# Neighbourhood attention on 416 keys a query tile in place of 512, its latent tokens stored by grid column, with turned edges of 32 queries, a third output tile begun early and one eviction moved ahead

## The reference

```python
def neighbourhood_attention(q, k, v, kc, vc, rpb):      # 16 heads of 64; kc, vc: 256 context tokens
    n_rows = S // GRID_W                                # 256 // 64 = 4, so kr = 4: all rows are seen
    q_cols = np.arange(GRID_W).reshape(n_cb, NA_QCOLS)
    win_start = np.clip(q_cols - NA_COLS // 2, 0, GRID_W - NA_COLS)   # 16 columns around the query
    ...
    s = jnp.where(col_valid, q_k * scale + bias, NEG_INF)
    s_ctx = jnp.einsum('bjqhd,bkhd->bhjqk', qr, kc) * scale
    p = softmax_f32(jnp.concatenate([s_ctx, s], -1))
    return p[..., :n_ctx] @ vc + p[..., n_ctx:] @ vb
```

## Time and profile before

| | us |
|---|---|
| median of three runs | 1891.6 |
| the profiled execution's own time | 1889.94 |
| its span, first to last instruction | 1888.2 |
| TensorE busy | 1735.9 (92%) |
| VectorE busy | 935.7 (50%) |
| ScalarE busy | 371.4 (20%) |

### The profile page before, as it was taken

The page is one execution under the profiler, slowest core; times in us unless marked ns, Lnnn a source line. Parts: engine busy times, 40 slices in busy tenths (PEclk is TensorE's granted clock), DMA queues, the critical chain, the costliest instruction groups (busy, mean ns, idle before and its releaser), DMA issues.

```text
span 1888.2 us, 33088 instructions
## 1 busy us (share of the span) xinstructions
PE 1735.9 (92%) x14018; PEld 1356.1 (72%) x14018; DVE 935.7 (50%) x1988; ACT 371.4 (20%) x884; POOL 0.2 (0%) x4
## 2 busy tenths in 40 slices
PE   7999999999999999999999999999999776667676
PEld 4455686888888887666888888788888655545554
DVE  1488878666667428788454412477433211111112
ACT  0343413121120014222211102212412100000001
POOL 0000000000000000000000000000000000000000
PEclk9999999999999999999999999999999988888888
DMA  9523342222231216654244543322296999999997
GB/s 384 207 113 125 144 179 71 79 80 86 86 145 36 109 47 207 205 184 173 90 163 149 208 171 134 134 81 121 90 380 267 426 427 428 429 428 429 428 428 314
DMA packets 35968, 395.72 MB, mean 210 GB/s; under 512 B 4000, under 2 KB 7072, under 8 KB 14368
## 3 DMA queue, kind: packets, MB, share of 16 engines
q1 hardware_dynamic: 35872, 394.33, 52.6%
HBM read 393.26 MB, written 1.05 MB: 209 GB/s over the span
## 4 chain that ended last, share of the span: by engine, by line
PE 78%; DMA 18%; DVE 2%; ACT 1%; issue 1%; SPq 0%; DVEq 0%; ACTq 0%
PE bank L636 19%; DMA arena<-w_moe 16%; PE bank L1918 13%; PE bank L1627 9%; PE bank L689 5%; PE bank L3683 3%; PE bank L2168 3%; PE bank L2214 2%; PE bank L934 2%; PE bank L3449 1%; PE bank L2164 1%; DMA ring<-w_moe 1%; PE bank L1235 1%; PE bank L843 1%; PE bank L2226 1%; PE bank L2775 1%
## 5 line engine op out<-in xcount | busy, mean ns | idle before, releaser
L636 PE MATMUL bank<-layer_input,ring 128*128 128x256 f32 x1152 | 253.1, 380 | 0.0
L636 PEld LDWEIGHTS bank<-layer_input,ring 128*128 128x128 f32 x1152 | 217.4, 190 | 31.6 <-issue 2.7
L3683 PE MATMUL bank<-arena 128*32 128x128 f32 x2008 | 82.1, 331 | 49.0 <-DMA arena<-w_moe 48.7
L1627 PE MATMUL bank<-arena,ring 128*128 128x256 f32 x544 | 121.7, 379 | 0.0
L3835 DVE TENSOR_TENSOR arena<-arena,bank 128x128 f32<-128x128 f32 x32 | 9.2, 288 | 218.4 <-PE bank L3683 218.4
L1918 PE MATMUL bank<-arena 128*128 128x256 f32 x504 | 115.7, 379 | 0.0
L3683 PEld LDWEIGHTS bank<-arena 128*32 128x32 f32 x2008 | 69.7, 134 | 62.0 <-DMA arena<-w_moe 59.0
L1627 PEld LDWEIGHTS bank<-arena,ring 128*128 128x128 f32 x544 | 103.2, 190 | 14.4 <-issue 0.4
L1918 PEld LDWEIGHTS bank<-arena 128*128 128x128 f32 x504 | 95.7, 190 | 13.2 <-DVE arena L2047 0.2
L689 PE MATMUL bank<-arena,ring 128*128 128x256 f32 x452 | 99.1, 380 | 0.9 <-DVE arena L2410 0.6
L689 PEld LDWEIGHTS bank<-arena,ring 128*128 128x128 f32 x452 | 85.6, 190 | 13.3 <-issue 1.0
(11 more groups left out here) (519 smaller groups left out, 2742.1 us busy)
## 6 DMA issues: line engine op xcount, KB each, us to landing
arena<-w_moe SPq DMA_DIRECT2D x45, 2048.0 KB, 25.8
ring<-w_moe SPq DMA_DIRECT2D x45, 2048.0 KB, 26.5
ring<-w_ffn_in SPq DMA_DIRECT2D x22, 2048.0 KB, 8.1
ring<-w_proj SPq DMA_DIRECT2D x7, 3072.0 KB, 10.3
ring<-w_ada_late SPq DMA_DIRECT2D x8, 2560.0 KB, 9.3
ring<-w_ffn_out SPq DMA_DIRECT2D x7, 2816.0 KB, 9.4
ring<-w_na_pair SPq DMA_DIRECT2D x5, 2048.0 KB, 8.1
arena<-w_far SPq DMA_DIRECT2D x16, 512.0 KB, 5.8
```

The costliest lines, as they stand in the source:

```text
L636: last = pe.matmul(out, a, b, start=(k == 0), stop=(k == len(lhs) - 1))
L1627: last = eng.matmul(out, w[:, k * P:(k + 1) * P], x[:, k, :], start=(start and k == 0), stop=(stop and k == half - 1), skip_group_check=True)
L3683: ins = eng.matmul(bank[x][group[q], 0:P], xe[:, k, SLOTS * e:SLOTS * e + SLOTS], weight(e, first, last, (x * KT + k) * FE + q * P, P), st ...
```

## The change

- **Order of the latent tokens.** `split_out` of the first FFN writes the 256 latent columns of `self.A` so that column c and row r of the grid stand at 4c + r (before: 64r + c). ScalarE's output of those 8 activations now steps by 4 elements. `attended` puts them back: VectorE's copy of each pair's output reads the bank in steps of 4.
- **416 keys.** Query tile 0 is now grid columns 0 to 31, tile 1 columns 32 to 63. With the context each tile sees 256 + 160 keys: the 40 grid columns nearest to it. Scores of tile 0 are one product of 416 columns; of tile 1 one of 160 and one of 256. VectorE's and ScalarE's steps on scores and exponentials take 416 columns where they took 512; the bias is 160 wide where it was 256.
- **Turning.** Each tile is now three full transposes and one edge: of the fourth block of 128 keys only the 32 queries at the border are turned, by a plain product with 32 partitions (96 to 127 for tile 0, 0 to 31 for tile 1), 128 weight columns and 32 moving columns of the identity. The 96 columns that no query writes are set to zero once, by two memsets on VectorE.
- **Attending.** Two blocks of context keys on 256 queries, then for each query tile one block on its 128 queries and one on the 32 at its border.
- **Bias and mask.** Two transfers where there were four, and two small ones for the mask, which leaves the constants (256 columns fewer).
- **Third output tile.** Tile 2 goes to bank 7 and no longer waits for `y_used`. Half of its sources (4 of 8) are multiplied ahead, directly behind `attend(7)`.
- **Mixer.** Group 21 is evicted ahead of `exponents(7)`.

The core of the diff:

```diff
+GRID_H = 4
+NEAR, EDGE = 160, 32
+SEEN = 256 + NEAR
...
+        home = [bank[7 if oc == 2 and begun == 3 else oc % 2] for oc in range(KT)]
...
-                if oc >= 2:
+                if oc >= max(2, begun):
                     eng.wait_ge(s["y_used"], base + oc - 1)
-                for k in range(nk - 1 if oc < begun else 0, nk):
+                for k in range((nk - 1, nk - 1, nk // 2)[oc] if oc < begun else 0, nk):
...
+                    to, of = self.A[:, k, c], x[:, c]
+                    if o["by_columns"] and seg:
+                        to, of = to.rearrange("p (c r) -> p r c", r=GRID_H), of.rearrange("p (r c) -> p r c", r=GRID_H)
...
+    def na_seen(self, p, n):
+
+        lo = (T - SEEN) * (n % 2)
+        return p[:, n, lo:lo + SEEN]
...
-                pe.matmul(bank[self.NA_SCORE_BANK[n]][:, :], v["q"][r, t * P:(t + 1) * P], v[f"k{u % 2}"][r, :],
-                          start=True, stop=True).then_inc(s["scored"], 1)
+                b, qt, k = bank[self.NA_SCORE_BANK[n]], v["q"][r, t * P:(t + 1) * P], v[f"k{u % 2}"][r, :]
+                if t == 0:
+                    last = pe.matmul(b[:, 0:SEEN], qt, k[:, 0:SEEN], start=True, stop=True)
+                else:
+                    pe.matmul(b[:, 0:NEAR], qt, k[:, T - NEAR:T], start=True, stop=True)
+                    last = pe.matmul(b[:, NEAR:SEEN], qt, k[:, 0:CTX], start=True, stop=True)
+                last.then_inc(s["scored"], 1)
...
-                for b in range(4):
-                    last = pe.transpose(bank[self.NA_TURN_BANK[n]][:, b * P:(b + 1) * P], p[:, n, b * P:(b + 1) * P],
-                                        self.con("ident"))
-                last.then_inc(s["turned"], 1)
+                to, x, t = bank[self.NA_TURN_BANK[n]], p[:, n, :], n % 2
+                for b, lo in enumerate(((0, P, CTX), (CTX, CTX + P, P))[t]):
+                    pe.transpose(to[:, b * P:(b + 1) * P], x[:, lo:lo + P], self.con("ident"))
+                asks, edge = ((slice(P - EDGE, P), 3 * P), (slice(0, EDGE), 0))[t]
+                pe.matmul(to[:, 3 * P:3 * P + EDGE], x[asks, edge:edge + P], self.con("ident")[asks, asks],
+                          start=True, stop=True, skip_group_check=True).then_inc(s["turned"], 1)
...
-            for b in range(4):
+            heads = [slice(64 * h, 64 * h + 64) for h in range(2)]
+            for b in range(2):
                 for h in range(2):
+                    pe.matmul(bank[6][heads[h], 0:LAT].rearrange("p (t q) -> p t q", t=2), vv[:, b, heads[h]],
+                              pt[:, h, :, b * P:(b + 1) * P], start=(b == 0), stop=False, skip_group_check=True)
+            for t in range(2):
+                for h in range(2):
+                    pe.matmul(bank[6][heads[h], t * P:(t + 1) * P], vv[:, 2 + t, heads[h]], pt[:, h, t, CTX:CTX + P],
+                              start=False, stop=False, skip_group_check=True)
+                for h in range(2):
+                    last = pe.matmul(bank[6][heads[h], P * t:P * t + EDGE] if t else bank[6][heads[h], P - EDGE:P],
+                                     vv[:, 3 - t, heads[h]], pt[:, h, t, 3 * P:3 * P + EDGE], start=False, stop=True,
+                                     skip_group_check=True)
...
         attend(7)
+        pe.wait_ge(s["vector_out"], self.na_steps(1, 1)["c12"])
+        out(2, range(KT // 2))
...
-            dve.tensor_copy(v["oT"][:, u * LAT:(u + 1) * LAT], bank[6][:, 0:LAT]).then_inc(s["o_used"], 1)
+            dve.tensor_copy(v["oT"][:, u * LAT:(u + 1) * LAT].rearrange("p (r c) -> p r c", r=GRID_H),
+                            bank[6][:, 0:LAT].rearrange("p (c r) -> p r c", r=GRID_H)).then_inc(s["o_used"], 1)
...
         queries(0)
+        halves = p.rearrange("p (h t) k -> p h t k", h=2)
+        dve.memset(halves[:, :, 0, SEEN:T], 0.0)
+        dve.memset(halves[:, :, 1, 0:T - SEEN], 0.0)
...
         evict(20)
+        evict(21)
         exponents(7)
-        evict(21)
```

More of the change, by code:

```diff
@@ L476, in biases, with na_mask @@
     def biases(self):
-        return self.N[:, 0:4096].rearrange("p (t h k) -> p t h k", t=2, h=8)
+        return self.N[:, 0:16 * NEAR].rearrange("p (t h k) -> p t h k", t=2, h=8)
+    def na_mask(self, t):
+        return self.N[:, (16 + t) * NEAR:(17 + t) * NEAR]
     def load_biases(self, sp, first, heads, loaded):
         src = slice(first + heads.start, first + heads.stop)
-        for row in range(4):
-            part = slice(64 * (row % 2), 64 * (row % 2) + 64)
-            sp.dma_start(self.biases()[part, row // 2, heads, :], self.nab_d[row][:, src, :]).then_inc(loaded, 16)
+        for t in range(2):
+            sp.dma_start(self.biases()[:, t, heads, :], self.nab_d[t][:, src, :]).then_inc(loaded, 16)
     def load_opening(self, sp):
@@ L688, in project @@
                     o = ((oc % per_chunk) * nk + k) * P
-                    last = eng.matmul(bank[oc % 2][:, 0:w], self.ring[g % 2][:, o:o + P], rhs(k), start=(k == 0),
+                    last = eng.matmul(home[oc][:, 0:w], self.ring[g % 2][:, o:o + P], rhs(k), start=(k == 0),
                                       stop=(k == nk - 1))
@@ L752, in residual @@
                     part = slice(CTX * seg - c0, CTX * seg - c0 + CTX)
-                    last = eng.scalar_tensor_tensor(out=h[oc][:, part], in0=bank[oc % 2][:, part],
+                    last = eng.scalar_tensor_tensor(out=h[oc][:, part], in0=home[oc][:, part],
                                                     scalar=self.ADA[:, layer, gate * KT + oc, seg:seg + 1],
@@ L2253, in out @@
             for k in ks:
-                pe.matmul(bank[oc][:, 0:LAT], self.ring[go % 2][:, (oc * KT + k) * P:(oc * KT + k + 1) * P], oT[:, k, :],
+                pe.matmul(bank[(0, 1, 7)[oc]][:, 0:LAT], self.ring[go % 2][:, (oc * KT + k) * P:(oc * KT + k + 1) * P], oT[:, k, :],
                           start=(k == 0), stop=False)
@@ L2548, in soften @@
                     act.wait_ge(s["max_ready"], 2 * u + n // 2 + 1)
[L2549 removed]
+                act.activation(self.na_seen(p, n), v["sc"][:, n, :], ACT.Exp, bias=nb[:, n:n + 1], scale=1.0,
                                accum_out=rs[:, n:n + 1]).then_inc(s["exp_done"], 1)
@@ L4203, in lay_out @@
     wide[:, :, 48:79] = r[:, 4:11, :]
[L4204 to L4208, removed]
+    nab = np.empty((2, P, 17, NEAR), np.float32)
+    for half in range(2):
+        q, k = np.arange(P) + P * half, np.arange(NEAR) + (LAT - NEAR) * half
+        (qc, qr), (kc, kr) = divmod(q, GRID_H), divmod(k, GRID_H)
+        nab[half, :, 0:16] = wide[:, kr[None, :] - qr[:, None] + 3, kc[None, :] - qc[:, None] + GRID_W - 1].transpose(1, 0, 2)
+        start = np.clip(qc - 8, 0, GRID_W - 16)
+        nab[half, :, 16] = np.where((kc[None, :] >= start[:, None]) & (kc[None, :] < start[:, None] + 16), 0.0, NEG)
+    return W, vec, np.ascontiguousarray(xT), nab
 def kernel(**inputs):
```

42 lines of the change are left out of this document (18 added, 24 removed).

## The result

The kernel after took 1896.5 us (median of 9 runs, 1895.3 to 1897.78), the kernel before 1891.54 in the same session (9 runs, 1890.52 to 1892.56). The ratio is 1.0027, 95% interval 1.0018 to 1.0036: 5.0 us slower, where 4.0 were forecast. The profiled execution took 1896.5 us, its span is 1894.4 (before: 1889.94 and 1888.2).

The account below looks back on a forecast made before the run. Up to about 1450 us TensorE's work in order bounds the time, then the experts' weight stream. 9.2 + 0.5 - 2.2 - 1.4 - 1.5 - 0.6 = +4.0 us on the median 1891.6 gives 1895.6 us, range 1889.0 to 1900.0.

Parts of the forecast that it names:

- a turn: TensorE's transposes and edges of a pair: 3.29 us for 1.75, +1.54, paid in full in six turns (+9.2 us).
- turn 1: The turn of pair 1, where TensorE waits about 1.0 us today: those waits go, leaving +0.5 us.
- scores, a pair: A pair's score matmuls on TensorE: 1.40 us for 1.72 with heads side by side, -0.32 us a pair.
- attend, a pair: A pair's attend matmuls on TensorE: 1.52 us for 1.73, -0.20 us a pair.
- end of the stage: Pair 7 and output projection: shorter chain, waits filled by half of tile 2, gain 1.5 us with turn 7 included.
- group 21 ahead: Mixer: TensorE's 0.61 us wait for group 21 goes; gain 0.6 us, between 0 and 0.7.
- sum before the experts: All terms together, 9.2 + 0.5 - 2.2 - 1.4 - 1.5 - 0.6 = +4.0 us.
- The first rival: Turn: edges need no change of the array's division; six turns cost 2.8 us, total -3.6, 1888.0 us; chance 0.13.
- that the second load hides: Edges in the turn: second weight load hides behind the first matmul, 2.0 us less, 1893.6 us; no separate chance given.
- The rule weighed in the prediction: TensorE matmuls start and end strictly in program order; by it tile 1's half of the scores would be slow.
- The signs named beforehand: Profile after: turn 3.2 to 3.3 us, scores 1.6, attend 1.7, no wait on L2410 or L753 in the output projection.
- heads in a row: Rival, scores: tile 1's heads run one behind the other, 0.47 us a pair, +3.8, 1899.4 us; chance 0.17.

Follow-up runs that it names:

- high_edge: The kernel after, with the edge product taken over all 128 partitions instead of 32: 1886.64 us, ratio 0.9978 to the kernel before.
- edge_added: The kernel before, with only a 32-row product added behind each tile's four transposes: 1905.15 us, ratio 1.0072.
- full_turn: The kernel after, with each edge turned as a fourth full 128x128 transpose, 32 columns copied out: 1886.45 us, ratio 0.9975 to the kernel before.
- third_only: The kernel before, with only the third output tile begun in bank 7 at the end of the heads: 1888.8 us in a single run, for 1891.39.
- edges_last: The kernel after, with the same four 32-row edge products behind all twelve transposes of the turn: 1887.65 us, ratio 0.9983 to the kernel before.

## Why the prediction was right, step by step

| step | forecast | measured |
|---|---|---|
| a turn | 3.29 us, +1.54 | 3.29, +1.54 |
| turn 1 | +0.5 | +0.32 (-0.11 + 0.22 + 0.21) |
| scores, a pair | -0.32 | -0.21 |
| attend, a pair | -0.20 | -0.22 |
| end of the stage | -1.5 | -1.38 |
| group 21 ahead | -0.6 | -0.70 |
| sum before the experts | +4.0 | +4.48 |

The measured terms make 6 x 1.54 + 0.32 - 7 x 0.21 - 7 x 0.22 - 1.38 - 0.70 = +4.47, and the run began the stage 0.09 early. That sum and forecast lie 0.48 apart is in part luck: the scores missed by +0.77 and the end by +0.12, while turn 1, the attend and group 21 came out 0.18, 0.14 and 0.10 lower.

*The turn.* The mechanism was the one forecast, and the size came out because each part came from a row: 0.09 in and 0.09 out from the earlier trace rows, the exposed loads from the earlier trace rows. The way in (0.09) and the whole edge (0.43) measured as forecast. The experiments give the sum its two halves: the product costs 0.19 us by itself (high_edge), the round trip of the division 0.31 on top of it. The first rival, that no division has to change, is refuted by high_edge and edge_added. Its price of 0.46 a turn was too high as well: in high_edge a turn is 2.06 - 1.75 = 0.31 longer than before. I had put each of the two passes at a load of 0.112 from the earlier trace rows, and one of them hides beside transposes. So the rival (that the second load hides) held on full height and not on 32 rows, where the forecast's 0.43 stood.

*The scores.* This is the term that was mis-sized, and with 7 x 0.11 = 0.77 us it is more than the whole of the sum's miss. I had allowed two answers: the heads stay side by side and the pair gains 0.32, or head 1's first product starts only behind head 0's second and the pair loses 0.15. TensorE by time, pair 3, has neither:

```profile
811.85 0.54 PE L2246 MATMUL bank<-arena 64*128 64x160 f32 x4
812.12 0.70 PE L2247 MATMUL bank<-arena 64*128 64x256 f32 x4
```

All four passes of the near parts (L2246), both heads', start before the far ones (L2247), though the program has head 0's far part ahead of head 1's near part. So the heads do run side by side. But head 1's first load isn't done ahead, and head 1 is 0.11 behind from there. The earlier trace rows show one product a head and could not show this. The rule weighed in the prediction (the Trainium skill, "TensorE: Matmul & The Clock Gate", Part 3, "The mechanism") is that matmuls keep the order of the program strictly and only weight loads are pulled ahead. The same rows speak against it: a product of another half of the rows did pass here, and it is the load that was late.

*The small ones.* Turn 1 cost 0.18 less than forecast: more of it fell into time in which TensorE had waited. The end gained 0.12 less. In full_turn, whose turn has its old length, it gains 2.62: about 1.17 of this is the third tile begun early (third_only), and the rest the shorter scores, softmax and attend. Turn 7's edges take 1.24 of it back. Group 21 gained the whole bound of 0.7. ScalarE's stepped writes got slower: 719 ns on the mean of 16, where half of them step, so about 0.85 for a stepped one if the others stayed at 0.59; TensorE waits 0.3 us for them once. VectorE's stepped reads of the output take 425 ns, about the 420 of L2405, which reads 256 unstepped columns.

*The end.* The median moved by 5.0, the experts' start by 4.4. I had taken what follows as a shift by the same amount. Two profiles of the kernel after, with the experts' start at +4.39 in both, end +5.0 and +6.2, so the stretch behind it differs by over 1 us between executions of one kernel. Another 0.3 us lies outside the span: I had added the 1.7 us of the kernel before, and in the kernel after the time is 2.0 us longer than the span on the median of nine runs (1.8 to 2.2). The runs of the kernels built on the kernel before have 1.8, so this comes with some part of the change; which one, no run shows.

*The signs named beforehand.* The turn takes 3.29 us (3.2 to 3.3 named), the scores 1.71 (1.6), the attend 1.66 (1.7), and the waits on L2410 and L753 are gone. Tile 1's scores take 0.81 us, under the 1 us that would have spoken for heads in a row.

## What to carry to other kernels

A product on a part of TensorE's rows between full ones costs a round trip of the array's division, 0.31 us here. With it an edge costs 0.50 us, where the full transpose that it replaces costs 0.11. A turn took 1.75 us with the whole block turned, and 2.06 with the product taken over all rows (the identity has zeros in the rest) as well as with the small ones gathered behind the large ones, for 3.29. Ask only then what the narrower data saves. And where two heads share the array, issue their products in turn, one of each, not one head's list behind the other's: 0.11 us a pair here on TensorE, not shown at the end of the kernel.

## What the runs showed of the hardware that was not expected

- Four edges one behind the other (eight matmuls on 32 rows, two row groups in turn) take 0.56 us together in edges_last; with transposes between them, in the kernel after, each edge takes 0.33, and the transposes behind it 0.15 more.
- A full transpose of 128 columns (0.109 us) is cheaper than a float32 product of 32 columns on full height (high_edge: two passes, 0.14, and 0.03 on the transposes behind it).
- With the edges last, all copies start later, and still neither engine's copies set the attend.
